# 64 fixed slots for each expert, gather and sums as high and low parts, and 4 MB of the second expert pair loaded into the dense ring

## What is computed

```python
p_group = softmax(xf @ wr_g + br_g); pg, gi = top_k(p_group, 1)          # 4 groups
e_in = the 8 expert logits of the chosen group
pv, pi = top_k(softmax(e_in), 2); gates = pg * pv / sum(pv)               # 2 of 8 experts
expert_id = gi * 8 + pi                                                   # 32 experts
for the tokens of each expert e:
    a, b = split(xb @ w_gu[e], 2)            # 1024 -> 2 x 512
    y = (silu(a) * b) @ w_down[e]            # 512 -> 1024
h = h + sum over the token's two experts of gate * y
```

```
layer 0: (1,4) (14,5) (5,7) (6,8) (12,5) (2,1) (6,8) (7,11) (12,68) (63,29) (17,78) (14,77) (1,8) (11,8) (6,3) (2,13)
layer 1: (10,7) (6,3) (12,9) (11,20) (20,27) (31,23) (24,21) (29,39) (14,4) (9,19) (8,13) (13,6) (26,8) (9,13) (23,22) (15,18)
```

## Time and profile before

| | us |
|---|---|
| median of 3 runs | 2206.72 (2201.84 to 2209.57) |
| the profiled execution's own time | 2208.49 |
| its span, first to last instruction | 2206.7 |
| TensorE busy | 2080.8 (94%) |
| weight loads on TensorE | 1519.7 (69%) |
| VectorE, ScalarE, GpSimd busy | 884.1 (40%), 687.7 (31%), 80.3 (4%) |
| DMA | 603.25 MB, 273 GB/s over the span |

### The profile page before, as it was taken

How to read it: one execution, slowest core, us unless ns; L and a number is a source line. 1 busy time by engine, 2 the same in 40 slices (tenths; PEclk the granted TensorE clock), 3 DMA queues, 4 the chain that set the end, 5 groups by cost and what they waited for, 6 DMA issues and landing times.

```text
span 2206.7 us, 37943 instructions
## 1 busy us (share of the span) xinstructions
PE 2080.8 (94%) x15688; PEld 1519.7 (69%) x15689; DVE 884.1 (40%) x1459; ACT 687.7 (31%) x1070; POOL 80.3 (4%) x119
## 2 busy tenths in 40 slices
PE   7997899998999998889999999989998999999998
PEld 5876899988999898744544444588987444444454
DVE  5866677755643544521111111156366111111112
ACT  3434455253553456511111111144342111111111
POOL 0110111101000200000000000000000000000000
PEclk9998999999999999989999999989998999999999
DMA  9731388912654251689999999625642899999992
GB/s 360 266 128 39 118 306 320 333 42 77 249 190 175 78 189 39 255 330 422 421 422 422 421 422 422 267 90 189 214 189 98 366 421 421 422 422 422 422 422 123
DMA packets 108115, 603.25 MB, mean 273 GB/s; under 512 B 10078, under 2 KB 10532, under 8 KB 58868
## 3 DMA queue, kind: packets, MB, share of 16 engines
q1 hardware_dynamic: 95872, 559.39, 64.0%
q0 software_dynamic: 11872, 42.35, 5.2%
q10 hardware_dynamic: 276, 0.13, 0.0%
HBM read 600.74 MB, written 1.05 MB: 273 GB/s over the span
## 4 chain that ended last, share of the span: by engine, by line
PE 85%; DVE 5%; ACT 4%; DMA 3%; issue 3%; SPq 0%; DVEq 0%; ACTq 0%
PE bank L945 20%; PE bank L957 10%; PE bank L552 10%; PE bank L553 9%; PE bank L554 9%; PE bank L929 6%; PE bank L976 5%; PE bank L582 4%; DMA dense_w<-in_w_in 1%; PE bank L562 1%; PE bank L563 1%; PE bank L561 1%; PE bank L632 1%; DMA dense_w<-in_mlp_w 1%; ACT w_high L428 1%
## 5 line engine op out<-in xcount | busy, mean ns | idle before, releaser
L945 PE MATMUL bank<-expert_w,work 128*32 128x512 f32 (+1 forms) x4032 | 446.1, 593 | 19.1 <-issue 19.1
L945 PEld LDWEIGHTS bank<-expert_w,work 128*32 128x32 f32 (+1 forms) x4032 | 156.7, 110 | 307.0 <-issue 307.0
L435 DVE TENSOR_TENSOR w_low<-dense_w,w_high 128x2048 fp32r<-128x2048 f32 x112 | 256.1, 2290 | 223.5 <-ACT w_high L428 222.9
L428 ACT ACTIVATE w_high<-dense_w 128x2048 fp32r<-128x2048 f32 x120 | 228.6, 1911 | 313.4 <-DMA dense_w<-in_mlp_w 197.6
L957 PE MATMUL bank<-expert_w,work 128*32 128x512 f32 (+1 forms) x2016 | 226.4, 594 | 0.0
L2092 DVE TENSOR_TENSOR work<-work,bank 128x512 f32<-128x512 f32 x32 | 22.0, 688 | 391.4 <-ACT work L1419 391.4
L929 PEld LDWEIGHTS bank<-work 128*128 128x128 f32 x1088 | 137.3, 205 | 43.9 <-issue 43.9
L957 PEld LDWEIGHTS bank<-expert_w,work 128*32 128x32 f32 (+1 forms) x2016 | 63.6, 110 | 144.4 <-issue 144.4
L929 PE MATMUL bank<-work 128*128 128x128 f32 x1088 | 143.7, 293 | 13.9 <-issue 7.7
L552 PE MATMUL bank<-u_pairs_mlp,w_high 128*128 128x256 f32 x512 | 146.1, 285 | 7.3 <-ACT u_pairs_mlp L1144 5.9
L553 PE MATMUL bank<-u_pairs_mlp,w_low 128*128 128x256 f32 x512 | 145.6, 284 | 0.0
(11 more groups left out here) (387 smaller groups left out, 3610.3 us busy)
## 6 DMA issues: line engine op xcount, KB each, us to landing
expert_w<-in_expert_w_gu SPq DMA_DIRECT2D x256, 1024.0 KB, 13.5
expert_w<-in_expert_w_down SPq DMA_DIRECT2D x128, 1024.0 KB, 9.8
dense_w<-in_mlp_w SPq DMA_DIRECT2D x64, 1024.0 KB, 5.3
dense_w<-in_ret_w_in SPq DMA_DIRECT2D x24, 1024.0 KB, 5.3
u<-in_ada_w POOLq DMA_DIRECT2D x40, 512.0 KB, 6.0
work<-in_ada_w POOLq DMA_DIRECT2D x40, 512.0 KB, 7.0
dense_w<-in_fox_w_in SPq DMA_DIRECT2D x16, 1024.0 KB, 5.1
dense_w<-in_w_in SPq DMA_DIRECT2D x12, 1024.0 KB, 7.9
```

Source lines behind the costliest of these rows:

```text
L428: nc.scalar.activation(HIGH_OF[at], dense_w[:, at % RING], ACT.Copy, scale=scale).then_inc(S("w_high_ready"), 1)
L435: ins = nc.vector.tensor_tensor(w_low[:, at % RING], dense_w[:, at % RING], high, ALU.subtract)
L945: last = mm(free[half][cols, :], rows[:, k, cols], pieces[:, k // 2, a, k % 2, half * 512:(half + 1) * 512], start=k == 0, stop=k == KT - 1)
```

## The change

What it does: each expert has 64 rows of the pair's 128, always; an expert with more than 64 tokens makes its pair run further rounds. The code for units, shares and fits goes, and with it the three variants of `project` and `down`; `project` has instead, for its first 4 k, one variant that reads the dense ring (pair 1) and one that reads `pieces`. `hn_tok` becomes a high and a low part, in permuted columns so that weights are contiguous; `gather` runs 32 single-pass products instead of 16 full ones. y is scaled by its row's gate (`slot_w`) when it leaves the bank and becomes a high and a low part, `pickT` holds 0 and 1; `add_up` runs 16 single-pass products. ScalarE makes both high halves of y behind a wait for `pick_wT_ready`, VectorE both low ones behind ScalarE. Behind the first pair's loads SyncE issues the up-projection's first two pieces of pair 1 (4 MB) into the dense ring in both layers; in the first iteration pieces 0 and 1 are refilled for pair 2, in halves of 64 partitions. All of retention's `ret_in` is issued behind layer 0's loop. The load of `ffn_gain` on GpSimd's queue moves behind the loads of `ada_w`.

```diff
@@ SyncE
+            def load_ahead(l):
+                for j in range(2):
+                    for a in range(2):
+                        sp.dma_start(dense_w[:, 2 * j + a].rearrange("p r n -> p (r n)"), rows_of(l, 1, j, a)).then_inc(S("expert_ahead"), 16)
...
-                if l == 0:
-                    for j in range(RING):
-                        load(chunk("ret_in", 0, j))
-                with sp.Fori(1, PAIRS) as i:
+                load_ahead(l)
+                for pair in range(2):
+                    for j in range(PIECES // 2):
+                        if (pair, j) in ((1, 0), (1, 1)):
+                            continue
+                        sp.wait_ge(expert_used, PIECES * (PAIRS * l + pair) + 2 * j + 2)
+                        load_experts(l, pair + 2 if j < 2 else pair + 1, j, 2 if j < 2 else 1)
+                with sp.Fori(3, PAIRS) as i:
...
-                    for at in range(chunk("ret_in", 1, 0), chunk("ret_out", 0, 0)):
+                    for at in range(chunk("ret_in", 0, 0), chunk("ret_out", 0, 0)):
@@ TensorE
-                            last = mm(free[2 + half][:, (k % 4) * P:(k % 4 + 1) * P], every_other(hn_tok[:, tt], k),
-                                      source[:, tt, :], start=tt == 0, stop=tt == TT - 1)
+                            for x in (hn_high, hn_low):
+                                last = mm(free[2 + half][:, (k % 4) * P:(k % 4 + 1) * P], x[:, tt, k * P:(k + 1) * P], source[:, tt, :],
+                                          start=tt == 0 and x is hn_high, stop=tt == TT - 1 and x is hn_low)
...
+                    with pe.If(i == 1):
+                        pe.wait_ge(S("expert_ahead"), 64 * (l + 1))
+                        for k in range(4):
+                            block_of(k, lambda a: dense_w[:, k // 2 * 2 + a])
+                    with pe.If(i != 1):
+                        for k in range(4):
+                            both_in(k, loaded)
+                            block_of(k, lambda a: pieces[:, k // 2, a])
+                    for k in range(4, KT):
...
-                        last = mm(total[k // 2][:, (k % 2) * SEQ:(k % 2 + 1) * SEQ], y_sb[:, k * P:(k + 1) * P],
-                                  pick_wT.rearrange("p t n -> p (t n)"), start=False, stop=False)
+                        for y in (y_high, y_low):
+                            last = mm(total[k // 2][:, (k % 2) * SEQ:(k % 2 + 1) * SEQ], y[:, k * P:(k + 1) * P], pickT,
+                                      start=False, stop=False)
...
-                    for first in SHARES:
-                        with pe.If(first_rows == first):
-                            project(xg, loaded, expert_used, first)
+                    project(i, xg, loaded, expert_used)
@@ ScalarE
+                for q in range(4):
+                    fn(hn_part(hn_high, q), bank(TILES[f"hn_{l}"] + q)[:, :], ACT.Copy, scale=small[:, 88 + q % 2:89 + q % 2]).then_inc(S("hn_high"), 1)
...
-                    fn(y_sb[:, 0:512], free[2][:, :], ACT.Copy).then_inc(done, 1)
+                    for half in range(2):
+                        fn(y_high[:, half * 512:(half + 1) * 512], free[2 + half][:, :], ACT.Copy, scale=slot_w).then_inc(done, 1)
...
+                    act.wait_ge(S("pick_wT_ready"), (PAIRS + 1) * l + i + 2)
                     take_y(S("y_act"))
@@ VectorE
-                V.memset(y_sb[:, 512:1024], 0.0).then_inc(S("y_dve"), 1)
+                V.tensor_scalar(y_low, const[:, 0:D], 0.0, None, ALU.mult).then_inc(S("y_dve"), 1)
...
+                low_of_hn(0)
+                low_of_hn(1)
...
+                crowd, more, upto = (share[:, b, :] for b in range(3))
+                V.tensor_copy(crowd, counts[:, 0, :])
+                evac(V.tensor_tensor(crowd, crowd, counts[:, 1, :], ALU.max), t)
...
                 link(V.tensor_scalar(more, crowd, float(SLOTS), None, ALU.is_gt))
...
-                link(V.tensor_scalar(fit, fit, -1.0, 1.0, ALU.mult, ALU.add))
-                link(V.tensor_tensor(more, more, fit, ALU.mult))
...
-                    V.tensor_copy(pick_wT, free[1][:, 0:SEQ].rearrange("p (t n) -> p t n", t=TT)).then_inc(done, 1)
+                    V.tensor_reduce(slot_w, free[1][:, 0:SEQ], AX.X, ALU.add)
+                    V.tensor_scalar(pickT, free[1][:, 0:SEQ], 0.0, None, ALU.is_gt).then_inc(done, 1)
...
+                def take_y(made, at, done):
+                    for half in range(2):
+                        dve.wait_ge(made, at + half + 1)
+                        eight = slice(half * 512, (half + 1) * 512)
+                        last = V.scalar_tensor_tensor(y_low[:, eight], free[2 + half][:, :], slot_w, y_high[:, eight].bitcast(f32),
+                                                      ALU.mult, ALU.subtract)
```

167 lines of the change are left out of this document (70 added, 97 removed).

## The result

The changed kernel takes 2290.61 us (2285.63 to 2292.15, 4 runs) against 2208.14 us of the kernel before beside it (2201.84 to 2224.53, 4 runs): a ratio of 1.0356, 95% interval 1.0319 to 1.0392. The forecast was 2267 with a range of 2233 to 2292; the measured time lies 1.4 us inside the upper end of that range and outside the forecast's own 2250 to 2284. The direction and the mechanism of the loss were right; the rounds cost more than forecast, and two gains that the sum contained (the first iteration and the load ahead) did not come as worked out.

What follows compares the result with a forecast made beforehand. TensorE sets the pace at 29.57 us an iteration, DMA right behind at 29.8. Rounds +113, layer 0 -29.8 and -2, layer 1 -17, router and sums -3.6: +60.6 us on 2206.72, so 2267 us, range 2233 to 2292.

Steps and rivals of the forecast that it cites:

- rival of costly rounds: Layer 0's further rounds: each 45 us and more, by slower clock or waits counted too short; 2289 or above, chance 0.13.
- signs of being wrong: No second up-projection in any iteration, a round shorter than 30 or longer than 45 us, or TensorE waiting in layer 0.
- layer 0 besides: Layer 0 without its rounds, bound by TensorE: 16 iterations each 1.86 us shorter, -29.8, and the first iteration's -2.
- all the rest: Router's chain and last adding up: shorter path from counts to pick, less longer y setup; -1.8 us a layer, -3.6.
- The rival on the other side: No rounds: a routing without an expert over 64, layer 0 bound by DMA too; 2167 us, chance 0.04.
- The round, 37.7 us: One further round in layer 0's pairs 8, 10, 11: 36.2 us built from steps plus 1.5 for slower clock; times 3, +113.
- Regular iteration, 27.7: One pair's iteration on TensorE: 29.57 us less 1.86, from split gather (0.32) and split sums (1.54).
- the rival of 0.067: Cheap gather: its products 0.067 us apart instead of 0.114, 28 us less in layer 0, 4 in layer 1; 2235, chance 0.2.
- First iteration, -2: Layer 0's first iteration: half of the 4.04 us of issue ahead of the first gather goes.
- Layer 1, -17: Layer 1 becomes bound by DMA, with 4.19 MB (9.94 us) less after the first release; ends at 2164 to 2168, not 2182.9.
- up to 5.8 if the hole of the first iteration remains: Layer 1's first two iterations: DMA's pauses grow by 1.8 us, up to 5.8 with that hole, delaying the last landing.
- load ahead without effect: DMA is not layer 1's limit or the pieces collide; layer 1 gains only 7 us, total 2277, chance 0.06.

Runs made afterwards that it cites:

- b_slots: The kernel before with one edit: no pair counts as fitting other than 64 + 64, so three old-form further rounds run; 2304.03 us, ratio 1.0440.
- i_two: The changed kernel with shares of 32 or 64 rows for the first expert, two variants of each projection, no further rounds; 2193.18 us, ratio 0.9914.
- j_two: i_two without the load ahead (SyncE's order as before the change); 2192.94 us, ratio 0.9908.
- o_best: i_two with the load ahead's refills in halves by columns instead of by partitions; 2186.53 us, ratio 0.9888.
- g_once: The changed kernel with one turn instead of three of the loops over further rounds on TensorE, ScalarE and VectorE; 2282.92 us, ratio 1.0303.
- h_warm: The changed kernel with 37 extra unused products in each further round, placed where TensorE waits; 2282.07 us, ratio 1.0307.
- e_noahead: The changed kernel without the load ahead (SyncE's order and the project as before the change); 2276.25 us, ratio 1.0273.
- d_ahead: The kernel before with the load ahead alone (SyncE's new order and the variant on the dense ring); 2903.83 us, ratio 1.3144.
- p_pad: c_split with 96 more products at the end of the further round's block, which no pair enters; 2527.34 us, ratio 1.1428.
- c_split: The kernel before with the split gather and sums alone, its own shares and order of loads; 2204.57 us, ratio 0.9986.
- a_fit: The changed kernel with the kernel before's adaptive shares (32, 64 or 96 rows, three variants of both projections); 2936.1 us, ratio 1.3311.
- n_cols: The changed kernel with the two refills for pair 2 cut into halves by columns instead of by partitions; 2280.85 us, ratio 1.0321.

## Why the prediction was right, and where it was not

The loss is the three further rounds, in the pairs that were named, and each was built from the right steps; that is why the direction held. The time itself came out at the edge of the range: it is where the rival of costly rounds stood (2289 or above, chance 0.13), though the rounds came to 44.4 us, just under that rival's 45. Of the signs of being wrong one came true: TensorE did wait for DMA in layer 0.

| term | forecast | measured |
|---|---|---|
| three further rounds | +113 (82 to 135) | +133.0 |
| layer 0 besides | -29.8 - 2 | -33.7 |
| layer 1 | -17 | -13.3 |
| all the rest | -3.6 | -4.2 (not to be told from the spread there) |
| span | +60.6 | +81.8 |

**What bounds, and the inputs.** Right: rounds in pairs 8, 10 and 11 and nowhere else. b_slots shows that the rounds by themselves cost 117 us in the old form, and i_two, j_two and o_best, with the split parts and no rounds, are all faster than before. The rival on the other side (no rounds, 2167) was right in its sign for a kernel without rounds and 20 us too cheap.

**The round, 37.7 us, was mis-sized: 44.4.** By its own steps in pair 8: to the gather 5.2 us (4.8 forecast), to the up-projection 10.8 (9.85), its end 26.5 (23.8), down-projection's start 29.8 (27.0) and end 36.9 (34.0), and 41.8 at the pair's own project, where the forecast had 36.7 with 0.5 for branches and took 0.5 off for the regular gap. The step that failed is "branches 0.5": it was 2.72 us, of which g_once shows 1.5 as two empty turns of the loop. The second is the clock: I put 1.5 us for it, and it was 1.7 in the round's project, 2.2 behind, and 1.6 in the sums of pairs 10 and 11. "No single hole of a round is over 2.7 us" was the argument against the costly rounds; the longest is 2.72, and the holes together with the clock behind them did it. The bound of 45 held.

**Regular iteration, 27.7, was 27.15.** The gather's 3.72 us confirm the router's pace of 0.114 (here 0.116 a product); the rival of 0.067 falls. By the Trainium skill's 81 ns ("TensorE: Matmul & The Clock Gate", "Back-to-back issue gap") it would have been 2.6 us, an estimate; the trace disagrees. The sums' 1.91 us were forecast as 1.92. The rest, 0.55 us, are the 64-row tiles (b_slots: 28.88 against 29.57), where I read that the tenth iteration "takes the same 13.96 and 7.02 us" from its two projections and not from the gap behind them. 16 times that is 9 us more of gain in layer 0, of which DMA took back about 5: TensorE did wait in layer 0, against the forecast. The waits of TensorE ahead of up-projections in layer 0 up to the first round (us in total, times, longest); the first row is the issue of the first iteration, the second the waits for DMA in pairs 5 to 7:

```profile
PE bank L959 <- issue: 5.5, 2, 3.0
PE bank L959 <- DMA expert_w<-in_expert_w_gu: 4.5, 4, 1.3
```

27.15 is under DMA's 29.8 us by 2.65 a pair, and by these rows the lead of the first pieces is used up after five pairs. "The rounds give DMA 113 us of rest" is true only behind the first round.

**First iteration, -2.** The hole ahead of the second gather went, but 5.45 us came ahead of the first up-projection (L959, the first row above), where before were 1.8. As said above, this hole goes with the variant on the dense ring, which the forecast left out of this term. Its size varies: it was 7.63 us in h_warm and 4.9 in g_once, which differ from the change only in the round's block. The first iteration as a whole, its two gathers included, takes 38.9 us instead of 41.9; 1.9 of these 3.0 us are the regular gain, so that about 1 us came where 2 were forecast. I had no ground for a sign here.

**Layer 1, -17, was -13.3, and not by the mechanism named.** "Its bytes after the first release fall by 4.19 MB: 9.94 us at 422 GB/s" failed at the rate: the refills go at 220. The step is "the halved transfers of two pieces: nothing", a term put at nothing with the reason that they are needed late; what they cost is not a wait of their own but 9.2 us of DMA time. And "up to 5.8 if the hole of the first iteration remains" was in the right place, as the end hangs on the first releases: the hole with its cold up-projection cost 6.1. That DMA ends the layer held: the last down-projection ends 9.1 us behind the last landing (2257.4, 2266.5), 7.1 forecast. e_noahead shows that the gain of layer 1 is the split parts and the 64-row tiles (-18.9 without the load ahead), and that the load ahead takes 5.5 of it back, by its first iteration. The rival "load ahead without effect" (0.06) was right that it brings nothing, though for another reason, and its -7 for the layer was not: the rest of the change gave more.

**The change as a whole.** The forecast costed the shares and the load ahead apart. The runs show that they hang together: the load ahead's second variant doesn't fit into the kernel before beside its three variants (d_ahead, +31%); dropping shares, and paying three rounds, makes the room. Dropping one of three variants makes it too, without a round for these inputs.

**Open.** The exact length and placing at which the loop is fetched anew; why the round's project is at 15.66 us in three of three rounds of the change and at 13.97 in g_once; why the first iteration's holes differ in size between versions, and between i_two and o_best with the same code on TensorE. p_pad has two runs only, 5.6 us apart, with 323 us between it and c_split.

## What to carry over

In a loop on the chip, count the code of all variants, also of those never entered, before adding one: here the 96 products that nobody runs cost 323 us. A block that stands on the path with half a dozen waits costs its matrix work (27 us) and two thirds again; fill or shorten its waits, and give its loop no empty turns. In a stage that DMA ends, look at the first releases: a hole in the first iteration moves the end (6.1 us here), and cut transfers by columns, not by partitions. Before a total that fits is taken as proof, its parts are added up from the trace: here the program outside the stages alone moved by 12 us between versions.

## Not expected of the hardware

- A loop's code on TensorE above some length is fetched anew in each iteration: 140 KB, mostly 12 to 15 us of issue ahead of the first product and 3 to 7 us ahead of the gather (a_fit, d_ahead, p_pad).
- A transfer to 64 partitions moves 215 to 226 GB/s at a full DMA share, one to 128 partitions 422, also with 4 KB a partition (n_cols).
- 64-row column tiles take 13.73 us for an up-projection and leave no gap behind the down-projection; 32-row tiles take 13.94 us and leave 0.5.
- An empty turn of a loop over a block that is skipped costs TensorE 0.77 us (g_once: two of them less, and the hole is 1.53 us shorter).
- An up-projection of 64 records takes 13.7 to 14.0 us at a granted clock of 1.00 and 15.5 to 16.0 us where the granted clock is 0.87 to 0.90 (the change, g_once, h_warm, b_slots).
